# Keys and outputs of a gated linear recurrence turned by VectorE and DMA instead of TensorE

## The reference

```
h    = rms_norm(x) * (1 + scale) + shift
proj = h @ w_in                    # q, k, v, gate za of attention; qb, fb, ib, zb of the recurrence
ya   = window_attention(...) * silu(za)                 # window 128, with sinks
f    = lb + (1 - lb) * sigmoid(fb);  k = (1 - lb) * sigmoid(-fb)
for chunk:                                              # 4 heads of 128 x 128 state
    L     = cumsum(log f)
    o     = (q * exp(L)) @ S + A @ v                    # A: decayed causal q k^T
    S     = exp(L_last) * S + (k * exp(L_last - L))^T @ v
yb   = rms_norm(o) * silu(zb)
y    = sigmoid(h @ w_merge)_a * (ya @ w_proj_a) + sigmoid(...)_b * (yb @ w_proj_b)
out  = x + gate * (y @ w_out)
```

## Time and profile before

| | |
|---|---|
| median of 3 runs | 1558.33 us (1558.32 to 1558.43) |
| profiled execution, span | 1555.9 us |
| TensorE busy | 1527.1 us, 98% |
| VectorE busy | 787.0 us, 51% |
| ScalarE busy | 540.7 us, 35% |
| GpSimd busy | 826.0 us, 53% |
| DMA | 178.94 MB, mean 115 GB/s, one queue with 33.4% of 16 engines' time |

### The profile page before, as it was taken

How to read it: one execution, slowest core, us unless ns; L and a number is a source line. 1 busy time by engine, 2 the same in 40 slices (tenths; PEclk the granted TensorE clock), 3 DMA queues, 4 the chain that set the end, 5 groups by cost and what they waited for, 6 DMA issues and landing times.

```text
span 1555.9 us, 31655 instructions
## 1 busy us (share of the span) xinstructions
PE 1527.1 (98%) x13048; PEld 1243.0 (80%) x13048; DVE 787.0 (51%) x1900; ACT 540.7 (35%) x1119; POOL 826.0 (53%) x1074
## 2 busy tenths in 40 slices
PE   5999999999999999999999999999999999999998
PEld 2777788877888788888779878888888978888886
DVE  4767464234558866232544774622453775623132
ACT  4334324334322532434331452243432353143330
POOL 0525434557863643365773472437786363437671
PEclk9999999999999999999999999999999999999999
DMA  9612211334453321233343231223544231222351
GB/s 339 243 55 83 83 57 55 111 133 158 168 197 108 110 70 57 82 109 108 137 164 135 92 120 43 83 66 114 208 154 149 75 110 56 78 72 91 102 167 60
DMA packets 62790, 178.94 MB, mean 115 GB/s; under 512 B 7086, under 2 KB 18695, under 8 KB 61864
## 3 DMA queue, kind: packets, MB, share of 16 engines
q1 hardware_dynamic: 62648, 176.93, 33.4%
HBM read 162.84 MB, written 11.96 MB: 112 GB/s over the span
## 4 chain that ended last, share of the span: by engine, by line
PE 95%; DVE 3%; DMA 1%; SPq 1%; issue 1%; ACT 0%; DVEq 0%
PE ps_D L758 56%; PE ps_D L755 25%; PE ps_XCD L820 2%; PE ps_XB L896 1%; PE ps_XB L949 1%; PE ps_XA L954 1%; PE ps_XA L921 1%; PE ps_XA L932 1%; PE ps_XB L948 1%; PE ps_XA L896 1%; DMA th_t<-in_w_ada 1%; SPq L507 1%; PE ps_XB L932 0%; PE ps_XCD L831 0%; PE ps_XCD L939 0%
## 5 line engine op out<-in xcount | busy, mean ns | idle before, releaser
L1702 POOL TENSOR_TENSOR w_lo_t<-w_raw,w_hi_t 128x256 fp32r<-128x256 f32 x920 | 681.0, 775 | 599.7 <-ACT w_hi_t L980 599.4
L758 PE MATMUL ps_D<-h_hi_t,w_hi_t 128*128 128x512 f32 x1024 | 411.2, 402 | 0.0
L758 PE MATMUL ps_D<-h_hi_t,w_lo_t 128*128 128x512 f32 x1024 | 399.6, 390 | 0.0
L758 PE MATMUL ps_D<-h_lo_t,w_hi_t 128*128 128x512 f32 x1024 | 399.5, 390 | 0.0
L980 ACT ACTIVATE w_hi_t<-w_raw 128x1024 fp32r<-128x1024 f32 x232 | 240.0, 1051 | 124.6 <-PE ps_D L755 61.6
L758 PEld LDWEIGHTS ps_D<-h_hi_t,w_hi_t 128*128 128x128 f32 x1024 | 192.3, 188 | 46.3 <-issue 8.9
L758 PEld LDWEIGHTS ps_D<-h_hi_t,w_lo_t 128*128 128x128 f32 x1024 | 192.2, 188 | 41.8
L758 PEld LDWEIGHTS ps_D<-h_lo_t,w_hi_t 128*128 128x128 f32 x1024 | 192.6, 188 | 36.5
L755 PE MATMUL ps_D<-w_hi_t,h_hi_t 128*128 128x384 f32 (+1 forms) x384 | 141.6, 369 | 1.0 <-DVE yf_t L1342 1.0
L755 PE MATMUL ps_D<-w_lo_t,h_hi_t 128*128 128x384 f32 (+1 forms) x384 | 136.6, 356 | 0.0
L755 PE MATMUL ps_D<-w_hi_t,h_lo_t 128*128 128x384 f32 (+1 forms) x384 | 136.3, 355 | 0.0
(11 more groups left out here) (386 smaller groups left out, 2332.9 us busy)
## 6 DMA issues: line engine op xcount, KB each, us to landing
w_raw<-in_w_blocks SPq DMA_DIRECT2D x232, 512.0 KB, 3.4
xr<-in_x_prompt SPq DMA_DIRECT2D x16, 512.0 KB, 5.0
x_or_AT<-in_x_prompt SPq DMA_DIRECT2D x14, 512.0 KB, 4.8
out_dram<-xr SPq DMA_DIRECT2D x12, 512.0 KB, 2.8
x_or_AT<-in_x_turned SPq DMA_DIRECT2D x3, 1024.0 KB, 5.6
p_or_hf<-in_x_turned SPq DMA_DIRECT2D x3, 1024.0 KB, 6.2
out_dram<-xr SPq DMA_DIRECT2D x8, 256.0 KB, 2.0
ibtok<-vtok SPq DMA_DIRECT2D x8, 192.0 KB, 3.5
```

Of the source, the lines that this page charges most:

```text
L758: ins = mm(bank[:, :], w[:, s0, k0 + k, :], a[:, k, :], start=go, stop=end)
L1702: ins = g_.tensor_tensor(w_lo[:, c, k:k + 2], w_raw[:, n % NRAW, k:k + 2], f32(w_hi[:, c, k:k + 2]), ALU.subtract)
```

## The change

The transposes on TensorE go. "kD" (half unit 56) lets VectorE transpose k in blocks of 32x32, in place, 256 tokens of all four heads per instruction; "ks" stores the result to scratch in device memory by a DMA that ScalarE issues, "kl" waits for it and issues four loads, which bring the 32x32 blocks back in transposed order, in rows of 32 floats (128 bytes), into `k_turned`. The outputs take the same way: "onorm" is split in two halves of 256 tokens, ends with the block transpose, then "os" stores, "ol" loads with four DMAs into `o_turned`, and "yD" multiplies by the gate. "o" and "st" stand at half units 60, 62, 64, 66 instead of 57, 59, 61, 63. Every half of keys or of outputs is 512 KB.

```diff
+KEYS_TURNED = (0, 1)
+O_AT, ON_AT, YD_AT, YT_AT = (60, 62, 64, 66), (63, 67), (69, 69, 71, 72), (70, 70, 72, 73)
+KS_AT, KL_AT, OS_AT, OL_AT = (56, 56), (57, 57), (65, 67), (67, 69)
...
     for _t in range(NT):
-        put(it, 28 + _t, 0, "KT", _t, "XC")
-        put(it, 28 + _t, 1, "o", _t, "XB")
-        put(it, 28 + _t, 1, "st", _t, "XA")
-    put(it, 32, 0, "onorm", 0)
+        if _t // 2 not in KEYS_TURNED:
+            put(it, 28 + _t, 0, "KT", _t, "XC")
+        at_half(it, O_AT[_t], "o", _t, "XB")
+        at_half(it, O_AT[_t], "st", _t, "XA")
+    for _r in KEYS_TURNED:
+        at_half(it, 56, "kD", _r)
+    for _r in range(2):
+        at_half(it, ON_AT[_r], "onorm", _r)
+        if _r in KEYS_TURNED:
+            at_half(it, KS_AT[_r], "ks", _r)
+            at_half(it, KL_AT[_r], "kl", _r)
+        at_half(it, OS_AT[_r], "os", _r)
+        at_half(it, OL_AT[_r], "ol", _r)
     for _t in range(NT):
-        at_half(it, 67 + _t, "yT", _t, "XB" if _t % 2 else "XA")
+        at_half(it, YD_AT[_t], "yD", _t)
+        at_half(it, YT_AT[_t], "yT", _t)
...
                 elif task == "st":
-                    s.freed(it, "KT", a)
+                    s.wait_ge(f"kt_in{a // 2}", 64 * (it + 1))
...
+                elif task == "ks":
+                    s.wait_ge("kD", len(KEYS_TURNED) * it + KEYS_TURNED.index(a) + 1)
+                    s.wait_ge(f"kt_in{a}", 64 * it)
+                    load(zk[a].rearrange("i q (h t) j p -> (i q) h (t j p)", t=2), kk[:, :, 256 * a:256 * a + 256], f"kz{a}")
+                elif task == "kl":
+                    s.wait_ge(f"kz{a}", 16 * (it + 1))
+                    for j in range(4):
+                        load(k_turned[32 * j:32 * j + 32, a].rearrange("p h t (i c) -> p (h t) i c", c=32),
+                             zk[a, :, :, :, j].rearrange("i q n p -> q n i p"), f"kt_in{a}")
+                elif task == "os":
+                    s.wait_ge("oD", 2 * it + a + 1)
...
+                elif task == "ol":
+                    s.wait_ge(f"oz{a}", 16 * (it + 1))
+                    s.full(it, "o" if a else "st", 3 if a else 1)
+                    for j in range(4):
+                        load(o_turned[a][32 * j:32 * j + 32].rearrange("p h t (i c) -> p (h t) i c", c=32),
+                             zo[a, :, :, :, j].rearrange("i q n p -> q n i p"), f"ot_in{a}")
...
+                elif task == "kD":
+                    half = kk[:, :, 256 * a:256 * a + 256]
+                    do(v.transpose(half, half), "kD")
                 elif task == "onorm":
-                    s.freed(it, "o", 3)
+                    s.freed(it, "o", 2 * a + 1)
...
+                    do(v.transpose(half, half), "oD")
-                elif task == "yT":
...
+                elif task == "yD":
+                    s.wait_ge(f"ot_in{a // 2}", 64 * (it + 1))
+                    do(stt(yf_slot(16 * it + 4 + a), o_turned[a // 2][:, :, a % 2], og_half[:, 0:1],
+                           szb[:, :, P * a:P * a + P], ALU.mult, ALU.mult), "yt")
```

More of the change, by code:

```diff
@@ L406, in build @@
         first.close()
+        k_turned = first.enter_context(nc.sbuf_tensor("k_turned", [P, 2, HB, 2, P], F32))
+        first.close()
+        first = ExitStack()
         yb_hi, yb_lo = sb("yb_hi_t", [P, 4, TB], F32R), sb("yb_lo_t", [P, 4, TB], F32R)
@@ L414, in build @@
         szb = qT
+        o_turned = [t.rearrange("p (h t n) -> p h t n", h=HB, t=2)
+                    for t in (acc_kst[:, :], qq.rearrange("p h n -> p (h n)")[:, 0:1024])]
+        zk, zo = (nc.dram_tensor(f"z_{n}", [2, 4, 32, 2 * HB, 4, 32], F32).ap() for n in "ko")
         y_hi, y_lo = sb("y_hi_t", [P, KT, TB], F32R), sb("y_lo_t", [P, KT, TB], F32R)
@@ L1001, in h_high_half, with load @@
                 s.done(fn(h_hi[:, k, P * t:P * t + P], hf[t % 2][:, k], ACT.Copy), "h_hi")
+            def load(dst, src, name):
+                s.done(act.dma_start(dst, src), name, by=16)
             s.wait_ge("x_in0", 16)
@@ L1124, in side @@
                     s.done(fn(esk, esk, ACT.Exp), "p_exp")
[L1125 to L1129, removed]
                 elif task == "o":
@@ L1169, in _ @@
                             if task == "yT":
-                                s.freed(it, "yT", a)
+                                s.full(it, "st", 3)
+                                s.wait_ge("yt", 4 * it + a + 1)
                                 high(yb_hi[:, :, P * a:P * a + P], 16 * it + 4 + a)
@@ L1547, in side @@
                     free(ins, *key)
+                elif task == "kD":
+                    half = kk[:, :, 256 * a:256 * a + 256]
+                    do(v.transpose(half, half), "kD")
                 elif task == "onorm":
-                    s.freed(it, "o", 3)
-                    do(ts(oss, oss, 1.0 / P, EPS, ALU.mult, ALU.add))
-                    rsqrt(orst, oss, ow1, ow2)
-                    for t in range(NT):
-                        o = kk[:, :, P * t:P * t + P]
[L1554 to L1558, removed]
+                    s.freed(it, "o", 2 * a + 1)
+                    c, half = slice(8 * a, 8 * a + 8), kk[:, :, 256 * a:256 * a + 256]
+                    do(ts(oss[:, c], oss[:, c], 1.0 / P, EPS, ALU.mult, ALU.add))
+                    rsqrt(orst[:, c], oss[:, c], ow1[:, c], ow2[:, c])
+                    for t in (2 * a, 2 * a + 1):
+                        o = kk[:, :, P * t:P * t + P]
+                        s.done(tt(o, o, orst[:, HB * t:HB * t + HB].unsqueeze(2).broadcast_to([P, HB, P]), ALU.mult))
+                    s.settle()
+                    do(v.transpose(half, half), "oD")
[3 more added lines that the diff above has]
+                           szb[:, :, P * a:P * a + P], ALU.mult, ALU.mult), "yt")
                 elif task == "rstd":
```

24 lines of the change are left out of this document (11 added, 13 removed).

## The result

| | before | after |
|---|---|---|
| median | 1558.32 us (1558.03 to 1558.43, 4 runs) | 1592.27 us (1590.29 to 1595.16, 4 runs) |
| ratio, 95% interval | | 1.0222 [1.0208, 1.0237] |
| profiled span | 1555.9 us | 1590.2 us |

Slower by 34.0 us, where 15.3 were forecast. The direction held, and the time lies within the outer range of 1556 to 1602, but above the forecast's own range of 1566 to 1586; the size is more than twice the forecast.

What follows compares the result with a forecast made beforehand. TensorE, busy 98%, was taken to bound the kernel. Span 1555.9 - 15.7 (groups removed) + 24.2 (waits) + 6.8 (clock) = 1571.2, plus 2.4 to the median: 1573.6 us; own range 1566 to 1586, outer 1556 to 1602.

Steps and rivals of the forecast that it cites:

- What bounds the kernel: TensorE, busy 98% of the span; only taking work off it helps, so far as it does not begin to wait.
- a group costs 0.49 us: Four transposes on TensorE plus the slower restart; removing 32 such groups of keys and outputs saves 15.7 us.
- The floor by GpSimd's order: Unit 35's weight split precedes the last two low parts of outputs on GpSimd: TensorE waits 17.2 us even with instantaneous DMAs.
- The trip: Outputs' store and loads through scratch on ScalarE's queue, with issuing holding ScalarE: last low part 5.9 us late.
- such meetings: Outputs' DMAs meeting 512 KB weight loads, which come every 5.4 us and occupy the engines 1.7 us: 0.5 us added.
- The term for waits: TensorE's new waits for outputs' low parts: 6.4 us in blocks 0, 2 and 3, 5.0 in block 1, 24.2 in all.
- The clock: TensorE's clock may drop to half speed after each of four new gaps: 1.7 us each, 6.8 in all.
- The keys: Turned keys land at 12.8 us, before TensorE asks at 15.4: hidden; at 27 ns a piece 0.5 us late per block.
- The sum: Whole kernel's span: 1555.9 - 15.7 + 24.2 + 6.8 = 1571.2 us; runs' median 2.4 above, 1573.6 us.
- GpSimd's order alone: Rival, 25%: quick loads at 9 ns a piece, waits stay at 17.2 us, one or two clock drops: 1560 to 1566.
- Small pieces cost as much as 512 B ones: Rival, 17%: loads of 128 B pieces take 27 ns each, outputs 10.0 us late: 1601 us.
- Faster after all: Rival, 12%: outputs' last low parts do not delay TensorE, the full 15.7 us saving shows: 1542.6 us.

Runs made afterwards that it cites:

- experiment 5: Changed kernel with keys turned by TensorE as before, only outputs by DMA, and "o" back at half units 57, 59, 61, 63: 1557.7 us, ratio 1.0.
- experiment 4: Changed kernel with 36, 22, 40 and 26 spare matmuls filling TensorE's four waits for the outputs: 1581.59 us, ratio 1.015.
- experiment 3: Changed kernel with the outputs' loads reading the same bytes in rows of 4 KB instead of 128 B, y wrong: 1584.71 us, ratio 1.0172.
- kernel 9: Kernel before the change with 96 spare transposes of 9 columns at TensorE's start: 1559.79 us, ratio 1.0016.

## Why the prediction was right in direction and wrong in size

- **What bounds the kernel; a group costs 0.49 us.** Right: 7.7 us for the sixteen groups of the outputs in experiment 5.
- **The floor by GpSimd's order, 17.2.** Right in kind and size: 18.9 with no trip. It is not 17.2 because the split takes 3.1 to 3.5 us in that kernel (3.7 in the changed one), not 2.82: VectorE is at work beside it (1447.36 against the earlier trace rows).
- **The trip.** This is the step that failed most: "so the store lands at X+13.9", and "ScalarE is held by issuing the second set until about X+16.3". It held in block 3 (X+14.1, X+16.9). In block 2 the store was through at X+16.0 and ScalarE held until X+20.4, in block 0 three loads alone took 5.20 us to issue. An issue was costed at 0.6 us, from issues of 512 pieces; the median was 0.71 and the longest 3.73, while SyncE's queue was moving. "I add 0.5 for such meetings" stood for the meetings with weight loads; the waits came out 3.3 and 4.5 us longer than forecast in blocks 0 and 2, and 0.8 and 1.0 in blocks 1 and 3. The term for waits was 24.2 and measured 33.8. (Block 1's 5.0 is not what the working gives: 6.4 less 1.0 is 5.4, and the sum 24.6.)
- **The clock.** Right mechanism, 6.8 forecast, 8.7 measured, 7 of it shown by experiment 4.
- **The keys.** Forecast as hidden, with 0.5 us a block at 27 ns a piece: 1.7 us of waits in three blocks, which are part of the 2.3 us missing in units 28 to 36. Both sets were issued together, eight issues in a row, and took 9 us (8.75 to 9.04).
- **A missing term.** Nothing in the prediction asked what it means to TensorE's program that 32 matmuls go in each block. 6.7 us hung on where its stops fall, a fifth of the loss, and that has nothing to do with how keys and outputs are turned: 36 spare transposes at the start take it away. The term stood at nothing.
- **The sum.** The span is 19.0 us over the forecast's 1571.2. Measured less forecast, the terms are: waits 9.6, stops 6.7, groups and keys 2.3, clock 1.9, the start -1.7.
- **Rivals.** "GpSimd's order alone" gave the floor but not the time. "Small pieces cost as much as 512 B ones" came nearer in us (1601) than the forecast, for a wrong reason: a piece took 13.0 ns, not 27. By luck its long landings stood in for the long issues. "Faster after all" fell at the waits.

What stays open: whether SyncE's loads, kept out of the way, would leave the issues short. The packets say that the long issues meet them, and experiment 3 that fewer pieces help (issues of 0.44 instead of 0.71 us, the longest 1.36 instead of 3.73, and 9 us less of waits); no run kept the two apart.

## What to carry to other kernels

A transfer in the middle of a chain costs its landing, the time that its issuing engine is held, and all that stands behind it on that engine; place it where the slowest landing seen, not the median, is covered, and look at what else moves on the DMA engines while it is issued. Where two things are late for the same instruction (GpSimd's order and the trip), removing one shows little. Before a small gain or loss is laid to an edit, look at stops without a releaser in runs of short instructions, and see if spare instructions at the start move them.

## What the runs showed of the hardware

- TensorE's instructions come in packets of about 16.4 KB (row "q8 instruction: 102, 1.67": 1.67 MB over 102), one to some 253 of its 25840 instructions (12920 matmuls, each with a load of weights into the engine). Late in a run of 96 or 128 short matmuls TensorE can stop for 0.6 to 1.9 us; two such stops in block 1 of the changed kernel stand 511 matmuls apart, about four times 128. The Trainium skill ("Runtime: NRT & Kernel Launch", Instruction fetch mechanics) has blocks of 256 instructions, with which the places agree, and says that the fetch is hidden; here it is not where matmuls are short: the 23 stops end 1.25 to 1.46 us after such a packet has landed.
- A stop of 1.76 us behind such a run was followed by a granted clock of 0.77 in the next 7.3 us (kernel 9), and the 2.7 us of its two stops cost 5.15 in all.
- A block transpose of 128x1024 takes VectorE 1.25 us; a DMA packet of 128 B takes 13.0 ns, one of 512 B 27.2, one of 1 KB 48, one of 4 KB 192 (means in the changed kernel).
- A load issue of 1024 pieces holds ScalarE for 0.6 to 0.7 us, and for up to 3.73 (7.57 for three in experiment 5) where many earlier pieces of its queue are unfinished and SyncE's queue is moving data.
- A weight split of four instructions takes GpSimd 2.82 us alone and up to 3.76 beside VectorE's work; two gate products take VectorE 1.54 us alone and 2.31 to 2.84 beside such a split.
